# A twelfth 2 MB weight slot, a smaller ring for dynamic DMAs, and a wait moved, in a one-core hybrid decoder step

## The chip, the cores and the metric

The kernel runs on one NeuronCore of a Trainium2 chip. The metric is the device time of one execution in microseconds. A core has TensorE (PE, with its weight loads PEld), VectorE (DVE), ScalarE (ACT), GpSimd (POOL) and SyncE (SP), and 16 DMA engines that all queues share. Here SP starts nearly all the large transfers, and POOL the indirect ones, which gather or scatter rows by a table of numbers (the dynamic DMAs, queue q0).

## The reference, cut to what matters

520 tokens (512 of a prompt, 8 single samples) of width 1024 go through one layer in float32.

```python
z = rmsnorm(x) @ w_in                      # split into xa, ga, ub, vb (512 each)
y_a = gelu(ssm(xa)) * sigmoid(ga)          # state space, 32 groups, complex diagonal state
y_b = gelu(ub) * spatial_gate(rmsnorm(gelu(vb)))
x = x + concat(rmsnorm(y_a), rmsnorm(y_b)) @ w_out
# mixture of experts: one of 4 groups, two of its 8 experts per token
for e in range(32):
    a, u = t @ w_gate[e], t @ w_up[e]      # (1024, 512) each
    out = out + combine[:, e:e+1] * ((silu(a) * u) @ w_down[e])   # (512, 1024)
y = rmsnorm(x + out)                       # plus the new states and the v rows
```

The experts' weights are 32 x 3 x 2 MB = 192 MB, and each of them is read once.

## The kernel before, in words

**Front (to about 241 us).** The projections, the state-space mixer, the gating mixer, the output projection and the router. Its buffers lie in one large tensor `mem`, cut by word offsets: `at_word(at, ...)`, `view(at, ...)` from word 24576 on, and `early` and `small` near the end of it, for the router's tables. Four input weights and two halves of `w_out` pass through slots 6 and 7.

**Weight slots.** `ring` divides the first 45056 words of `mem` into NSLOT = 11 slots of UNIT = 4096 words (16 KB in each of 128 partitions, 2 MB). One unit is half of an expert's gate and up weights, or its whole down weight. `UNITS` lists the 96 units in the order in which PE wants them, and unit q goes into slot q modulo NSLOT. SP loads a slot as soon as the front has left it: units 0 to 5 and 8 with the front's last part, 6, 7, 9 and 10 (in pieces) while the output projection's buffers come free. Unit NSLOT and the one behind it come in pieces as PE has used up slots 0 and 1 (`load_piece`, with the semaphores `gu_part`, `gu_half`, `gu_ps`); from then on `load(q)` waits until PE has used unit q - NSLOT (`gu_half`, `gu_ps` or `dn_ps`).

**Experts.** For each expert in turn, 64 tokens at a time: POOL gathers the tokens' rows from DRAM (`fetch`, two experts ahead), PE turns them, multiplies by gate and up, ACT applies silu, DVE multiplies, PE turns the result and multiplies by down, ACT copies it out, and POOL scatters it to `y2_d` in DRAM (`store`). PE computes expert s's gate and up before expert s - 1's down. Experts with more than 64 tokens take further tiles (`further`). PSUM tensors psA and psB alternate.

**The last two experts** are not scattered: their rows are added by a product with a selection matrix `picks`, which DVE makes once, early (`picks_of`, L1256), from `tokens`, numbers that lie in the same words as ACT's output buffer `yst`. It needs `cw_ps`, a small product that PE does in the middle of expert 1's gate and up. ACT waits for it (`picks_rdy`) before it starts expert 1, and PE before it starts expert 2.

**Zeroes.** `y2_d` is first filled with zeroes, 4 MB, by SP at L368 and L369; ACT waits for that before L627, whose output lies on the zero buffer.

**End.** After the stream, SP reads residuals (`x2f`), scattered rows (`yin`) and the final gain (`gfb`) into slots that are free by then; DVE and PE add and scale, and SP writes the result.

SP runs its waits and its DMA issues strictly in the order of the program. The lines that matter:

```python
def load(q):
    e, j = UNITS[q]
    s = q % NSLOT
    unit(s, (ring[:, s, :], w_dn[e] if j == 2 else w_gu[2 * e + j]))
for q in range(NSLOT + 2, 3 * NE):
    e_old, j_old = UNITS[q - NSLOT]
```

Of the kernel before, what the change touches and what calls it, by code (L numbers as in the profile page):

```python
# [7 lines left out]
D = 1024  # L8
DS = 512
NP_, NS = 512, 8  # L10
NTOK = NP_ + NS
NT = 5
# [14 lines left out]
NSLOT, UNIT = 11, 4096  # L27
FRONT_SLOTS = 6
ARENA = FRONT_SLOTS * UNIT
EPS = 1e-6  # L30
# [11 lines left out]
def build(nc, a, o):  # L42
# [3 lines left out]
    with ctx:  # L46
        def sb(name, shape, dt=f32):
            return ctx.enter_context(nc.sbuf_tensor(name, shape, dt))
# [70 lines left out]
        hnew = at_word(49152, 2, NS, NQ)  # L119
# [68 lines left out]
        thr = small(270, 8)  # L188
        one32 = small(278, NE)
        ex = small(310, NT, NG + 1)  # L190
        row_oh = as_bf16(small(376, NT * C)).rearrange("p (t j c) -> p t j c", t=NT, j=2)
        oh12 = small(696, NT, 2, NE)
        brb = small(336, 36)
# [11 lines left out]
        vi = sb("vi", [128, C])  # L205
        iot = vi[:, :]
        rank_at = early(1160, C)
        ids = cut(1792, 4, 2 * NE)
        ohb = sb("ohb", [128, NT, 32], bf16)
        trib = sb("trib", [128, 128], bf16)  # L210
        oneb = sb("oneb", [128, 128], bf16)
# [4 lines left out]
        picks = small(376, NP_ + 32)  # L216
        tokens = cut(0, NTOK)[64:128]
        x2_root = tiny[:, 0:20].rearrange("p (t w) -> p t w", w=4)
        of_last = small(1016, 2, NT, 2, 2)
        cw3 = as_bf16(small(1056, NT * 2 * 4)).rearrange("p (t j e w) -> p t j e w", t=NT, j=2, e=2)  # L220
        tok_cw = tiny[64:128, 92:96]
        WQ = D // 4
        xq, yq0, yq1, gfq = (at_word(2 * D + WQ * k, WQ) for k in range(4))
        cwq, sumq, rootq, scaleq = tiny[:, 20:22], tiny[:, 22:23], tiny[:, 23:24], tiny[:, 24:25]
        same_row = st[:, 0:32]
# [72 lines left out]
        def as8(s):  # L298
            return ring[:, s, :].rearrange("p (k n) -> p k n", k=KD)

        def as4(s):
            return ring[:, s, :].rearrange("p (k n) -> p k n", k=4)
# [42 lines left out]
        def _(sp):  # L345
            def unit(s, src):
                sp.dma_start(src[0], src[1]).then_inc(w_full[s], 16)
# [6 lines left out]
            unit(7, (ring[:, 7, :], a["w_xa"]))  # L354
            sp.wait_ge(vbp_ps, 1)
            unit(6, (ring[:, 6, :], a["w_ga"]))
            sp.wait_ge(xa_ps, 4)
            unit(7, (ring[:, 7, :], a["w_ub"]))
            sp.wait_ge(ga_ps, 4)
            unit(6, (ring[:, 6, :], a["w_out"][1]))  # L360
# [9 lines left out]
            sp.wait_ge(ub_ps, 4)  # L370
            unit(7, (ring[:, 7, :], a["w_out"][0]))

            def load(q):

                e, j = UNITS[q]
                s = q % NSLOT
                unit(s, (ring[:, s, :], w_dn[e] if j == 2 else w_gu[2 * e + j]))

            def load_blocks(q, k0, k1):

                e, j = UNITS[q]
                s = q % NSLOT
                words = slice(2 * DE * k0, 2 * DE * k1)
                unit(s, (ring[:, s, words], (w_dn[e] if j == 2 else w_gu[2 * e + j])[:, words]))
# [15 lines left out]
            sp.wait_ge(s_ev, NH)  # L400
            sp.dma_start(g2, a["norm2_g"]).then_inc(rest_in, 16)
# [35 lines left out]
            def load_piece(q, n):  # L437

                e, j = UNITS[q]
                s = q % NSLOT  # L440
                k0, k1 = PIECES[s][n]
                sp.dma_start(ring[:, s, 2 * DE * k0:2 * DE * k1],
                             (w_dn[e] if j == 2 else w_gu[2 * e + j])[:, 2 * DE * k0:2 * DE * k1]).then_inc(w_full[s], 16)
# [55 lines left out]
        def _(act):  # L499
# [202 lines left out]
            def tile_step(s, i, u, before=True):  # L702

                ps, other = (psA, psB)[u], (psA, psB)[1 - u]
                x0 = act.value_load(xb[0:1, bass.ds(s, 1)], min_val=0, max_val=NX)
                x1 = act.value_load(xb[0:1, bass.ds(s + 1, 1)], min_val=0, max_val=NX)
                further(x0, x1, other)
                act.wait_ge(gu_ps, s + 1)
                A(sg[64:128, u, :], ps[0:64, 1, :], ACT.Silu, scale=root_of[0:64, u:u + 1]).then_inc(sg_rdy, 1)  # L709
                if before:  # L710
                    tail(s - 1, i, 1 - u)

            def tail(s, n_stored, u):
# [60 lines left out]
        def _(dve):  # L774
# [472 lines left out]
            tile_step(0, 0, early=True)  # L1247
            dve.wait_ge(zero_out, 32)
# [11 lines left out]
            tile_step(1, 1)  # L1260
# [20 lines left out]
            def add_rows(t):  # L1281

                dve.wait_ge(y_in[t], 48 if t < 4 else 64 + 128)
                acc, rows, by = ((x2f[:, t, :], yin[:, 2 * t:2 * t + 2, :], cw[:, :, t]) if t < 4
                                 else (xq, at_word(2 * D + WQ, 2, WQ), cwq))
# [39 lines left out]
        def _(pool):  # L1325
# [8 lines left out]
            def tt(out, x, y, op):  # L1334
# [17 lines left out]
            link(G.memset(trib[:, :], 1.0))  # L1352
            G.memset(oneb[:, :], 1.0)
            G.affine_select(out=trib[:, :], in_=trib[:, :], compare_op=ALU.is_gt, fill=0.0, base=0,
                            pattern=[[1, 128]], channel_multiplier=-1)
            G.iota(iot, [[1, C]], base=0, channel_multiplier=0, allow_small_or_imprecise_dtypes=True).then_inc(iota_rdy, 1)
# [13 lines left out]
            G.memset(zeros, 0.0).then_inc(consts, 1)  # L1370
            pool.wait_ge(st_out, 16 * 5)
# [92 lines left out]
            G.memset(at_word(2 * D, 4 * WQ), 0.0).then_inc(tokens_rdy, 1)  # L1464
# [521 lines left out]
```

## Time and profile before

| | |
|---|---|
| median of 3 runs | 729.3 us (729.06, 729.3, 1117.75) |
| span of the profiled execution | 727.1 us |
| the profiled execution's own time | not recorded apart from its span; the two near runs are 2.0 and 2.2 us above the span |
| PE busy | 652.3 us (90%) |
| DVE, ACT, POOL busy | 255.7, 158.4, 97.2 us |
| moved by DMA | 244.48 MB, of which SP's queue 233.95 MB and the dynamic queue 8.24 MB |

The span runs from the first to the last instruction of the core, and all times in the traces count from its start. The chain of work that ended last passes through PE for 65% of the span, DVE and DMA 11% each. A busy PE is not a bound PE here: the slices of the page show, under PE, how full the DMA engines are, and the two have to be read side by side.

### The profile page before, as it was taken

The page shows a single profiled execution, that of the slowest core. Times are in us where ns is not written, and L with a number is a line of the kernel's source. Part 1 is how long each engine was busy: PE and PEld are TensorE (multiplying, and loading weights), DVE is VectorE, ACT ScalarE, POOL GpSimd, SP SyncE. Part 2 cuts the span into 40 slices and gives each one's busy share as a digit, 9 for nine tenths or more (in the row PEclk, how much of TensorE's full clock was granted, in tenths as well). Part 3 has the DMA queues.
Part 4 walks back from the last instruction along what each step waited for, and adds up shares of the span by engine and source line. Part 5 has one row for each costly group of instructions (what it writes and reads, how often), then busy time and mean ns, then how long its engine had stood idle before and what let it go on. Part 6 is the DMA issues. An engine that isn't in the chain of part 4 may idle for free.

```text
span 727.1 us, 9232 instructions
## 1 busy us (share of the span) xinstructions
PE 652.3 (90%) x3176; PEld 314.2 (43%) x3176; DVE 255.7 (35%) x553; ACT 158.4 (22%) x312; POOL 97.2 (13%) x165
## 2 busy tenths in 40 slices
PE   8999999999999999996899999987777778778994
PEld 5478888874456533332233333322222222223331
DVE  7798997188265612111010101110001100001047
ACT  3677511132322111110011111101001010001123
POOL 5100000000000311222012121212211112121000
PEclk9999999999999899998999999999999999999999
DMA  9532005569848699999999999999999999999993
GB/s 326 222 116 112 5 1 189 184 240 431 300 150 313 208 427 423 425 422 422 428 424 426 424 424 422 425 422 428 422 426 426 426 424 425 425 425 423 411 351 127
DMA packets 32692, 244.48 MB, mean 336 GB/s; under 512 B 7344, under 2 KB 8016, under 8 KB 19584
## 3 DMA queue, kind: packets, MB, share of 16 engines
q1 hardware_dynamic: 25592, 233.95, 78.3%
q0 software_dynamic: 5280, 8.24, 3.1%
q10 hardware_dynamic: 1768, 1.53, 0.7%
q8 instruction: 40, 0.66, 0.4%
q14 instruction: 12, 0.10, 0.0%
HBM read 235.76 MB, written 17.09 MB: 348 GB/s over the span
## 4 chain that ended last, share of the span: by engine, by line
PE 65%; DVE 11%; DMA 11%; another core or an unknown queue 4%; ACT 3%; issue 3%; SPq 1%; ACTq 0%; POOLq 0%; POOL 0%; DVEq 0%
PE psA L1480 33%; PE psB L1480 30%; DMA mem<-in_w_gu 7%; DVE mem L785 4%; DMA mem<-y_d 2%; DVE mem L1009 1%; DMA mem<-x_d,mem 1%; PE psB L1485 1%; ACT front_c L709 1%; DMA y_d<-mem 1%; PE psA L1485 1%; ACT mem L717 1%; DVE mem L924 1%; DVE mem L936 1%
## 5 line engine op out<-in xcount | busy, mean ns | idle before, releaser
L1480 PE MATMUL psA<-mem 128*128 128x260 f32 (+8 forms) x848 | 200.9, 476 | 7.8 <-DMA mem<-in_w_down 5.4
L1480 PE MATMUL psB<-mem 128*64 128x512 f32 (+6 forms) x710 | 153.5, 490 | 13.6 <-DMA mem<-in_w_down 4.7
L1480 PEld LDWEIGHTS psA<-mem 128*128 128x128 f32 (+4 forms) x848 | 108.0, 161 | 82.2 <-issue 61.4
L1480 PE MATMUL psB<-mem,front_c 128*64 128x512 f32 (+3 forms) x554 | 121.5, 577 | 15.9 <-DMA mem<-in_w_gu 15.9
L1480 PE MATMUL psA<-mem,front_c 128*64 128x512 f32 (+2 forms) x548 | 121.1, 581 | 15.5 <-DMA mem<-in_w_gu 13.5
L1480 PEld LDWEIGHTS psB<-mem 128*64 128x64 f32 (+3 forms) x710 | 73.7, 160 | 78.1 <-issue 57.3
L1480 PEld LDWEIGHTS psB<-mem,front_c 128*64 128x64 f32 (+2 forms) x554 | 41.2, 142 | 94.5 <-issue 67.8
L1480 PEld LDWEIGHTS psA<-mem,front_c 128*64 128x64 f32 (+1 forms) x548 | 40.6, 142 | 93.0 <-issue 69.5
L1184 DVE SCALAR_TENSOR_TENSOR front_c<-psA,tiny,front_c 64x512 f32<-64x512 f32 x16 | 12.1, 755 | 180.7 <-ACT front_c L709 168.0
L785 DVE TENSOR_TENSOR mem<-mem 128x512 f32<-128x512 f32 (+15 forms) x109 | 65.5, 615 | 23.8 <-ACT mem L616 19.6
L1184 DVE SCALAR_TENSOR_TENSOR front_c<-psB,tiny,front_c 64x512 f32<-64x512 f32 x16 | 12.1, 755 | 173.3 <-ACT front_c L709 166.6
L1392 POOL DMA_INDIRECT y_d<-front_c,mem x30 | 30.9, 1031 | 263.2 <-ACT front_c L720 263.2
L1387 POOL DMA_INDIRECT mem<-x_d,mem x34 | 36.5, 1072 | 92.4 <-DVE mem L785 64.4
L709 ACT ACTIVATE front_c<-psA,tiny 64x512 f32<-64x512 f32 x15 | 10.2, 682 | 119.2 <-PE psA L1480 119.2
L709 ACT ACTIVATE front_c<-psB,tiny 64x512 f32<-64x512 f32 x15 | 10.2, 682 | 114.8 <-PE psB L1480 114.8
L1485 PE MATMUL psA<-ident,mem 128*128 128x128 f32 (+1 forms) x128 | 19.1, 283 | 5.1 <-DMA mem<-x_d,mem 4.8
L720 ACT ACTIVATE front_c<-psA 128x512 f32<-128x512 f32 x15 | 9.0, 597 | 61.7 <-PE psA L1480 61.7
L720 ACT ACTIVATE front_c<-psB 128x512 f32<-128x512 f32 x15 | 9.0, 597 | 60.3 <-PE psB L1480 60.3
L1485 PEld LDWEIGHTS psA<-ident,mem 128*128 128x128 f32 (+1 forms) x128 | 13.9, 144 | 9.8 <-issue 7.7
L785 DVE TENSOR_TENSOR mem<-psB,mem 128x512 f32<-128x512 f32 (+2 forms) x23 | 15.0, 706 | 2.4 <-PE psB L1480 2.4
L1480 PE MATMUL psB<-ident 128*128 128x128 f32 x60 | 12.4, 391 | 3.0 <-POOL mem L1340 2.0
L1485 PE MATMUL psB<-ident,mem 128*128 128x128 f32 (+1 forms) x88 | 13.5, 279 | 1.7 <-DVE mem L1184 1.7
(260 smaller groups left out, 381.6 us busy)
## 6 DMA issues: line engine op xcount, KB each, us to landing
mem<-in_w_gu SPq DMA_DIRECT2D x61, 2048.0 KB, 35.2
mem<-in_w_down SPq DMA_DIRECT2D x30, 2048.0 KB, 37.5
mem<-in_w_out SPq DMA_DIRECT2D x2, 2048.0 KB, 8.4
y_d<-mem SPq DMA_DIRECT2D x1, 4096.0 KB, 11.8
mem<-y_d SPq DMA_DIRECT2D x8, 512.0 KB, 8.4
mem<-in_w_gu SPq DMA_DIRECT2D x6, 512.0 KB, 3.9
mem<-in_w_down SPq DMA_DIRECT2D x3, 1024.0 KB, 6.2
mem<-in_w_gu SPq DMA_DIRECT2D x3, 1024.0 KB, 7.1
```

Of the source, the lines that this page charges most:

```text
L709: A(sg[64:128, u, :], ps[0:64, 1, :], ACT.Silu, scale=root_of[0:64, u:u + 1]).then_inc(sg_rdy, 1)
L717: A(hT[:, u, :, :], ps[:, 2, 0:256].rearrange("p (k c) -> p k c", k=4), ACT.Copy).then_inc(hT_ev, 1)
L720: A(yst[:, u, :], ps[:, 3, :], ACT.Copy).then_inc(y_cp, 1)
L785: return V.tensor_tensor(out, x, y, op)
L924: V.tensor_copy(*u_copy(ql, e, 1))
L936: ins = V.scalar_tensor_tensor(v[:, hs], v[:, hs], st[0:r, 44 + 4 * t + h:45 + 4 * t + h], gmg[0:r, hs], ALU.mult, ALU.mult)
L1009: V.tensor_copy(mixA[32 * ql:32 * ql + 32, :, 0:NP_].rearrange("p m (b i) -> p i m b", i=T)[:, i], yg[32 * i:32 * i + 32, ql, :, NS:YC])
L1184: return V.scalar_tensor_tensor(out, up, root, silu, ALU.mult, ALU.mult)
L1387: return G.indirect_dma_start(out=dst, out_offset=None, in_=x2_d[:, :], in_offset=bass.IndirectOffsetOnAxis(ap=rows_ap, axis=0), bounds_ch ...
L1392: return G.indirect_dma_start(out=y2_d.rearrange("t (h n) -> (t h) n", h=2), out_offset=bass.IndirectOffsetOnAxis(ap=rows_ap, axis=0), in_ ...
L1480: return nc.tensor.matmul(out, lhsT, rhs, start=start, stop=stop, skip_group_check=True)
L1485: return nc.tensor.transpose(out, in_, ident[b0:b0 + p, b0:b0 + p])
```

## The change

NSLOT becomes 12. The twelfth slot (number 11) is not next to the others: it lies at word 49296, behind the tables, so `ring` becomes a list. Its 4096 words come from three sources: the software ring for dynamic DMAs is set to 2048 bytes of each partition (before, the default of 16384), some separate tensors (`st`, `vi`, `ohb`, `trib`, `oneb`) go into words of `mem` that are free at their time, and the tables are laid closer. The words of slot 11 hold `st` and `hnew` until the new state has been written out; then SP loads unit 11 there, right behind the zeroes and before the second half of `w_out`. What is pieced now are units 12 and 13. POOL makes `trib`, `oneb` and `iot` later, when `dec` is no longer used. DVE makes the selection after its step of expert 1 and not before, and ACT waits for it only before its first write of `yst`. SP waits for `h0_rdy` before it loads the router's biases. The buffers of the end move to slots 1 to 4; before, they lay in slots 8 to 10 and 0, and both sets hold units 85 to 88.

```diff
-NSLOT, UNIT = 11, 4096
+NSLOT, UNIT = 12, 4096
+LAST_SLOT = 49296
+RING_BYTES = 2048
-        mem = sb("mem", [128, ARENA + 24928])
-        ring = mem[:, 0:NSLOT * UNIT].rearrange("p (s n) -> p s n", n=UNIT)
+        mem = sb("mem", [128, LAST_SLOT + UNIT])
+        ring = [mem[:, at:at + UNIT] for at in [UNIT * s for s in range(NSLOT - 1)] + [LAST_SLOT]]
-        hnew = at_word(49152, 2, NS, NQ)
+        hnew = at_word(LAST_SLOT + 64, 2, NS, NQ)
-        gfb = at_word(0, D)
-        y_kept = at_word(D, D)
-        x2f = at_word(8 * UNIT, 4, D)
-        yin = at_word(9 * UNIT, 8, D)
+        gfb = at_word(4 * UNIT, D)
+        y_kept = at_word(4 * UNIT + D, D)
+        x2f = at_word(UNIT, 4, D)
+        yin = at_word(2 * UNIT, 8, D)
-        st = sb("st", [128, 64])
+        st = at_word(LAST_SLOT, 64)
...
@@ sync
             sp.dma_start(y2_d[1024:2 * NTOK, :], zeros[0:2 * NTOK - 1024]).then_inc(zero_out, 16)
-            sp.wait_ge(ub_ps, 4)
-            unit(7, (ring[:, 7, :], a["w_out"][0]))
...
+            sp.wait_ge(st_out, 16 * 5)
+            load(NSLOT - 1)
+            sp.wait_ge(ub_ps, 4)
+            unit(7, (ring[7], a["w_out"][0]))
...
             sp.wait_ge(s_ev, NH)
+            sp.wait_ge(h0_rdy, 2)
             sp.dma_start(g2, a["norm2_g"]).then_inc(rest_in, 16)
@@ scalar
-            def tile_step(s, i, u, before=True):
+            def tile_step(s, i, u, before=True, ahead=None):
...
                 stored(act, n_stored, u)
+                if ahead:
+                    act.wait_ge(*ahead)
                 A(yst[:, u, :], ps[:, 3, :], ACT.Copy).then_inc(y_cp, 1)
...
             tile_step(0, 0, 0, before=False)
-            act.wait_ge(picks_rdy, 1)
-            tile_step(1, 0, 1)
+            tile_step(1, 0, 1, ahead=(picks_rdy, 1))
@@ vector
             tile_step(0, 0, early=True)
+            tile_step(1, 1)
             dve.wait_ge(zero_out, 32)
             dve.wait_ge(tokens_rdy, 1)
             dve.wait_ge(cw_ps, 1)
...
             picks_of(0)
             picks_of(1).then_inc(picks_rdy, 1)
-            tile_step(1, 1)
             tile_step(2, 0)
@@ gpsimd
-            link(G.memset(trib[:, :], 1.0))
-            G.memset(oneb[:, :], 1.0)
...
             pool.wait_ge(s_ev, NH)
             G.memset(zeros, 0.0).then_inc(consts, 1)
+            pool.wait_ge(dec_used, 4)
+            link(G.memset(trib, 1.0))
+            G.memset(oneb, 1.0)
...
-    nc = bacc.Bacc("TRN2", target_bir_lowering=False, num_devices=1)
+    nc = bacc.Bacc("TRN2", target_bir_lowering=False, num_devices=1, dynamic_dma_scratch_size=RING_BYTES)
```

How SP's queue stands around the zeroes, before (`out` are the results, `y_d` is `y2_d`, `in_w_out` and `in_w_gu` weights):

```order
L366 DMA out<-mem 128x128
L368 DMA y_d<-mem 128x8x1024 [waits consts]
L369 DMA y_d<-mem 16x1024
L347 DMA mem<-in_w_out 128x4096 [waits ub_ps]
L401 DMA tiny<-in_norm_g 128x8 [waits s_ev]
L402 DMA mem<-in_b_router_group 128x4
L403 DMA mem<-in_b_router_expert 128x32
```

and in the changed kernel:

```order
L367 DMA out<-mem 128x128
L369 DMA y_d<-mem 128x8x1024 [waits consts]
L370 DMA y_d<-mem 16x1024
L348 DMA mem<-in_w_gu 128x4096 [waits st_out]
L348 DMA mem<-in_w_out 128x4096 [waits ub_ps]
L405 DMA tiny<-in_norm_g 128x8 [waits h0_rdy,s_ev]
L406 DMA mem<-in_b_router_group 128x4
L407 DMA mem<-in_b_router_expert 128x32
```

One weight load of 2 MB has come between the zeroes and `w_out`; it waits for `st_out`, which `w_out` is now behind too.

SP's queue where the slots are used for the second time, before (`gu_part`, `gu_half`, `gu_ps` and `dn_ps` count what PE has used):

```order
L347 DMA mem<-in_w_gu 128x1024 [waits xg_in0,x2_out]
L442 DMA mem<-in_w_gu 128x1024 [waits gu_part] x2
L442 DMA mem<-in_w_gu 128x2048 [waits gu_half]
L442 DMA mem<-in_w_gu 128x2048 [waits gu_part]
L442 DMA mem<-in_w_gu 128x2048 [waits gu_ps]
L347 DMA mem<-in_w_down 128x4096 [waits gu_half]
L347 DMA mem<-in_w_gu 128x4096 [waits gu_ps]
```

and in the changed kernel:

```order
L348 DMA mem<-in_w_gu 128x1024 [waits xg_in0,x2_out]
L446 DMA mem<-in_w_gu 128x1024 [waits gu_part] x2
L446 DMA mem<-in_w_gu 128x2048 [waits gu_half]
L446 DMA mem<-in_w_down 128x2048 [waits gu_part]
L446 DMA mem<-in_w_down 128x2048 [waits gu_ps]
L348 DMA mem<-in_w_gu 128x4096 [waits gu_half]
L348 DMA mem<-in_w_gu 128x4096 [waits gu_ps]
```

The waits stand as before, and behind each stands the unit that came one place later: the down unit of expert 3 where the second gate and up unit of expert 4 was, and so on to the end, which is one load shorter.

DVE's queue in experts 0 and 1, before: the selection (from the row that waits for `cw_ps`) stands right behind expert 0's product (the row that waits for `sg_rdy`):

```order
L1184 SCALAR_TENSOR_TENSOR front_c<-psA,tiny,front_c 64x512 [waits sg_rdy]
L1251 CAST tiny<-mem 64x2 [waits cw_ps,tokens_rdy,zero_out]
L1252 TENSOR_REDUCE tiny<-psB 64x2
L1256 TENSOR_SCALAR mem<-front_c,tiny 64x520 [waits dve_step]
L1256 TENSOR_SCALAR mem<-front_c,tiny 64x520
L1216 TENSOR_LOAD xb
```

and in the changed kernel, from expert 1's product on:

```order
L1189 SCALAR_TENSOR_TENSOR front_c<-psB,tiny,front_c 64x512 [waits sg_rdy]
L1199 COPY tiny<-mem 128x1 [waits xgT_ps]
L790 TENSOR_TENSOR front_c<-psA,tiny 128x512
L1257 CAST tiny<-mem 64x2 [waits cw_ps,tokens_rdy,zero_out]
L1258 TENSOR_REDUCE tiny<-psB 64x2
L1262 TENSOR_SCALAR mem<-front_c,tiny 64x520 [waits dve_step]
L1262 TENSOR_SCALAR mem<-front_c,tiny 64x520
L1221 TENSOR_LOAD xb
```

The selection's four rows have moved behind expert 1's product and behind the turned tokens of expert 2.

## Rows read from the trace of the kernel before

**Rows 1.** page, part 2: DMA share in tenths, GB/s; 40 slices
```profile
DMA  9532005569848699999999999999999999999993
GB/s 326 222 116 112 5 1 189 184 240 431 300 150 313 208 427 423 425 422 422 428 424 426 424 424 422 425 422 428 422 426 426 426 424 425 425 425 423 411 351 127
```

**Rows 2.** windows: stretch, length, busy us by engine (instructions), clock, DMA share, GB/s
```profile
136.00:144.00 8.00, 8.00 (x39) 6.92 (x38) 1.31 (x2) 1.13 (x2) 0.00 (x0) 1.00 0.01 2
...
241.00:246.00 5.00, 4.26 (x41) 3.40 (x42) 3.64 (x16) 0.00 (x0) 0.78 (x2) 0.78 0.41 119
246.00:250.00 4.00, 4.00 (x22) 1.39 (x20) 2.34 (x14) 0.00 (x0) 1.23 (x2) 1.00 0.69 201
250.00:682.00 432.00, 376.73 (x1796) 133.29 (x1794) 53.82 (x105) 52.51 (x95) 77.33 (x126) 0.98 1.01 424
```

**Rows 3.** windows: PE ahead of the weight stream, and behind it
```profile
262.00:330.00 68.00, 66.92 (x328) 23.54 (x324) 9.45 (x21) 8.91 (x16) 14.89 (x26) 1.00 1.01 425
...
500.00:676.00 176.00, 137.68 (x646) 48.00 (x644) 19.05 (x36) 19.16 (x35) 29.13 (x46) 0.99 1.01 425
```

**Rows 4.** waits of PE, 262:460: total us, times, longest
```profile
PE psA L1485 <- DMA mem<-x_d,mem: 4.8, 1, 4.8
```

**Rows 5.** waits of PE, 500:676
```profile
PE psB L1480 <- DMA mem<-in_w_gu: 16.5, 12, 2.5
PE psA L1480 <- DMA mem<-in_w_gu: 11.5, 10, 1.4
```

**Rows 6.** timeline of SP: start us, us, line, transfer
```profile
123.93 0.58 SPq L369 DMA_DIRECT2D y_d<-mem  x1
144.16 0.33 SPq L347 DMA_DIRECT2D mem<-in_w_out  x1
...
241.42 0.33 SPq L347 DMA_DIRECT2D mem<-in_w_gu  x1
246.12 7.07 SPq L442 DMA_DIRECT2D mem<-in_w_gu  x5
...
643.22 4.24 SPq L347 DMA_DIRECT2D mem<-in_w_down  x1
```

**Rows 7.** DMA queues (packets, MB), issues (KB each, us to landing)
```profile
q0 software_dynamic: 5280, 8.24, 3.1%
...
mem<-in_w_gu SPq DMA_DIRECT2D x61, 2048.0 KB, 35.2
...
y_d<-mem SPq DMA_DIRECT2D x1, 4096.0 KB, 11.8
...
mem<-x_d,mem POOLq DMA_INDIRECT x34, 8.9
...
y_d<-front_c,mem POOLq DMA_INDIRECT x30, 8.1
```

**Rows 8.** timeline of ACT: the first that waits for the zeroes
```profile
147.58 1.28 ACT L627 ACT_TABLE_LOAD   x1
```

**Rows 9.** timeline of POOL: its memset, then the rank table
```profile
122.53 0.95 POOL L1370 MEMSET mem<- 128x1024 f32 x1 [49.03 <-DVE mem L785]
173.40 0.16 POOL L1374 IOTA mem<- 128x32 f32 x1 [49.92 <-ACT mem L627]
```

**Rows 10.** timeline of DVE: selection rows, then expert 2's tokens
```profile
257.13 1.12 DVE L1256 TENSOR_SCALAR mem<-front_c,tiny 64x520 f32<-64x520 f32 x2
...
261.93 0.69 DVE L785 TENSOR_TENSOR front_c<-psA,tiny 128x512 f32<-128x512 f32 x1
```

**Rows 11.** timeline of PE: expert 0's down product
```profile
261.40 3.65 PE L1480 MATMUL psA<-mem 128*64 128x512 f32 x16 [0.22 <-ACT mem L717]
```

**Rows 12.** timeline of PE and POOL: last weight wait, last scatter
```profile
672.92 3.65 PE L1480 MATMUL psB<-mem 128*64 128x512 f32 x16 [1.46 <-DMA mem<-in_w_gu]
...
684.56 0.97 POOL L1392 DMA_INDIRECT y_d<-mem  x1 [15.28 <-ACT mem L700]
...
693.57 0.10 POOL L1474 MEMSET mem<- 128x1 int32 x1 [7.92 <-DMA y_d<-mem]
```

More of the change, by code:

```diff
@@ L187, in build @@
         Wp, Wq, Wr, Wm = (small(226 + 10 * k, NT, 2) for k in range(4))
[L188 to L193, printed above, removed]
+        thr = early(1400, 8)
+        one32 = early(1304, NE)
+        ex = early(1372, NT, NG + 1)
+        row_oh = as_bf16(small(268, NT * C)).rearrange("p (t j c) -> p t j c", t=NT, j=2)
+        oh12 = small(588, NT, 2, NE)
+        brb = early(1336, 36)
         xxg = at_word(46088, ROW)
@@ L215, in build @@
         ylast = y_kept[64:128]
-        picks = small(376, NP_ + 32)
+        picks = small(268, NP_ + 32)
         tokens = cut(0, NTOK)[64:128]
         x2_root = tiny[:, 0:20].rearrange("p (t w) -> p t w", w=4)
-        of_last = small(1016, 2, NT, 2, 2)
-        cw3 = as_bf16(small(1056, NT * 2 * 4)).rearrange("p (t j e w) -> p t j e w", t=NT, j=2, e=2)
+        of_last = early(1224, 2, NT, 2, 2)
+        cw3 = as_bf16(early(1264, NT * 2 * 4)).rearrange("p (t j e w) -> p t j e w", t=NT, j=2, e=2)
         tok_cw = tiny[64:128, 92:96]
         WQ = D // 4
-        xq, yq0, yq1, gfq = (at_word(2 * D + WQ * k, WQ) for k in range(4))
+        xq, yq0, yq1, gfq = (at_word(4 * UNIT + 2 * D + WQ * k, WQ) for k in range(4))
         cwq, sumq, rootq, scaleq = tiny[:, 20:22], tiny[:, 22:23], tiny[:, 23:24], tiny[:, 24:25]
-        same_row = st[:, 0:32]
+        same_row = early(1408, 32)
         psA = ctx.enter_context(nc.psum_tensor("psA", [128, 4, 512], f32))
@@ L298, in as8 @@
         def as8(s):
-            return ring[:, s, :].rearrange("p (k n) -> p k n", k=KD)
+            return ring[s].rearrange("p (k n) -> p k n", k=KD)
         def as4(s):
-            return ring[:, s, :].rearrange("p (k n) -> p k n", k=4)
+            return ring[s].rearrange("p (k n) -> p k n", k=4)
         def by_pair(ps):
@@ L353, in _ @@
                 sp.dma_start(x2[0:ROWS[t], t, :], xsrc(t)).then_inc(x_in[t // 3], 16)
-            unit(7, (ring[:, 7, :], a["w_xa"]))
+            unit(7, (ring[7], a["w_xa"]))
             sp.wait_ge(vbp_ps, 1)
-            unit(6, (ring[:, 6, :], a["w_ga"]))
+            unit(6, (ring[6], a["w_ga"]))
             sp.wait_ge(xa_ps, 4)
-            unit(7, (ring[:, 7, :], a["w_ub"]))
+            unit(7, (ring[7], a["w_ub"]))
             sp.wait_ge(ga_ps, 4)
-            unit(6, (ring[:, 6, :], a["w_out"][1]))
+            unit(6, (ring[6], a["w_out"][1]))
             sp.wait_ge(vbn, NT)
@@ L376, in load @@
                 s = q % NSLOT
-                unit(s, (ring[:, s, :], w_dn[e] if j == 2 else w_gu[2 * e + j]))
+                unit(s, (ring[s], w_dn[e] if j == 2 else w_gu[2 * e + j]))
+            sp.wait_ge(st_out, 16 * 5)
+            load(NSLOT - 1)
+            sp.wait_ge(ub_ps, 4)
+            unit(7, (ring[7], a["w_out"][0]))
             def load_blocks(q, k0, k1):
@@ L383, in load_blocks @@
                 words = slice(2 * DE * k0, 2 * DE * k1)
-                unit(s, (ring[:, s, words], (w_dn[e] if j == 2 else w_gu[2 * e + j])[:, words]))
+                unit(s, (ring[s][:, words], (w_dn[e] if j == 2 else w_gu[2 * e + j])[:, words]))
             def reuse_tile(n):
@@ L441, in load_piece @@
                 k0, k1 = PIECES[s][n]
-                sp.dma_start(ring[:, s, 2 * DE * k0:2 * DE * k1],
+                sp.dma_start(ring[s][:, 2 * DE * k0:2 * DE * k1],
                              (w_dn[e] if j == 2 else w_gu[2 * e + j])[:, 2 * DE * k0:2 * DE * k1]).then_inc(w_full[s], 16)
@@ L710, in tile_step, with tail @@
                 if before:
-                    tail(s - 1, i, 1 - u)
-            def tail(s, n_stored, u):
+                    tail(s - 1, i, 1 - u, ahead)
+            def tail(s, n_stored, u, ahead=None):
                 ps = (psA, psB)[u]
@@ L1370, in _ @@
             G.memset(zeros, 0.0).then_inc(consts, 1)
+            pool.wait_ge(dec_used, 4)
+            link(G.memset(trib, 1.0))
+            G.memset(oneb, 1.0)
+            G.affine_select(out=trib, in_=trib, compare_op=ALU.is_gt, fill=0.0, base=0,
+                            pattern=[[1, 128]], channel_multiplier=-1)
+            G.iota(iot, [[1, C]], base=0, channel_multiplier=0, allow_small_or_imprecise_dtypes=True).then_inc(iota_rdy, 1)
             pool.wait_ge(st_out, 16 * 5)
@@ L1463, in _ @@
             pool.wait_ge(dn_ps, NE - 3)
-            G.memset(at_word(2 * D, 4 * WQ), 0.0).then_inc(tokens_rdy, 1)
+            G.memset(at_word(4 * UNIT + 2 * D, 4 * WQ), 0.0).then_inc(tokens_rdy, 1)
             store(NE - 3, NE // 2 - 2, 1)
```

14 lines of the change are left out of this document (5 added, 9 removed).

## The prediction

> **What bounds the kernel now.** I read the slices of the page first. The DMA engines are full from the fourteenth slice on, at 422 to 428 GB/s [rows 1]. Before that they have gaps, two of them nearly empty slices. The windows give the same in us: from 250 to 682 us the engines move 424 GB/s without a gap [rows 2]. This is the stream of the experts' weights.
>
> Then I asked who waits for whom. Between 262 and 330 us PE is busy for 66.92 of 68 us [rows 3], and between 262 and 460 us its longest wait is one gather of 4.8 us; no weight stands in that answer ahead of it [rows 4]. PE lives on the slots that were filled before 241 us. Between 500 and 676 us it is busy for 137.68 of 176 us [rows 3], and of the 38.3 us left, 16.5 + 11.5 = 28.0 us are waits for gate and up weights [rows 5], most of the rest for down weights. So the stock of full slots is used up on the way, and from there each expert ends when its weights land. The last such wait ends at 672.92 us [rows 12]. What follows is a fixed tail of 727.1 - 672.9 = 54.2 us: two experts' products, the last scatter, which lands at 693.57 us [rows 12], the rows read back, the sum.
>
> That makes a short sum: end = start of the stream + bytes left at that time / 424 GB/s + tail. Only bytes moved before the stream starts, in time when the engines idle, take anything off it.
>
> **The twelfth slot.** It takes 2 MB (2.097 MB) out of the stream and moves it ahead. In the stream they cost 2.097 MB / 424 GB/s = 4.95 us [rows 2]; by the slices' 422 and 428 GB/s, 4.97 and 4.90 us [rows 1]. What do they cost in the new place? SP now issues the load after the zeroes, so at 123.93 + 0.58 = 124.5 us or a little later, when the small results have landed. The 4 MB of zeroes take 11.8 us from issue to landing [rows 7], until 135.7 us. From 136 to 144 us the engines move 2 GB/s: 8 us of idle time [rows 2]. The load needs 4.95 of them and is done by about 140.7 us. The next user, the second half of w_out, is issued at 144.16 us [rows 6], when the engines are empty again. Even if the wait for the results held the load until 139.2 us, it would fit. If reads and zeroes share the engines, the zeroes are late by at most 4.95 us, at 140.7 us; ACT, which waits for them, comes to that point at 147.58 us [rows 8], 6.9 us later. So this costs 0 at the lower end. The upper end, if cover were missing altogether, is the 4.95 us themselves; I take 0, because the idle row is measured at just this place.
>
> The Trainium skill has another rate (DMA: Bandwidth & Descriptors, "Where 436 GB/s comes from"): for HBM to SBUF it puts the limit at about 358 GB/s for a core. By that the unit would be worth 2.097 / 358 = 5.9 us, an estimate, and the time 723.4 us. The trace disagrees, with 424 GB/s over 432 us, and the measurement decides; the rule gets no chance of its own.
>
> **The restart of the stream.** The engines also idle from 241 to 246 us (119 GB/s) and are half loaded to 250 us (201 GB/s) [rows 2]. The extra slot does not fill this: it has long been full, and the first reuse waits, as before, for PE's first products of expert 0. SP's first piece went out at 246.12 us, right behind the last prefetch at 241.42 us [rows 6]. Gates, sizes and order of the issues are the same, each with the next unit. Cost and gain 0; the remaining stream is one load shorter.
>
> **Does PE follow?** It has 38.3 us of waiting between 500 and 676 us [rows 3] and needs to give back 4.95 us. The wait for expert 30's weights at 672.92 us moves to about 668.0 us, and the tail with it. SP's last load, now at 643.22 us [rows 6], and the rest of the stream move by the same amount, so the tail meets the same traffic as before.
>
> **The selection for the last experts.** DVE's two large rows take 1.12 us [rows 10], with the two small ones ahead of them I take 1.5 us. Before, they stood in a time when DVE waited for ACT. Now they follow expert 2's turned tokens, which end at 261.93 + 0.69 = 262.62 us [rows 10], so they end near 264.1 us. PE waits for them before expert 2, but until 261.40 + 3.65 = 265.05 us it does expert 0's down product [rows 11]: cover of about 0.9 us. ACT needs them before its copy of that same product, also after 265.05 us. Nothing is queued behind them on DVE that is needed before expert 2's gate and up end. Cost 0. If the cover were gone, a us or two of PE would be lost at a time when PE is ahead of the weights [rows 3, 4], which is made good later. I see no gain either, since the selection was done at 257.13 + 1.12 = 258.25 us [rows 10], before ACT had expert 1's products.
>
> **POOL's tables.** Four small instructions move to behind POOL's memset, which starts at 122.53 us and takes 0.95 us; POOL then waits 49.92 us, until 173.40 us [rows 9], and the first DVE reader also needs what POOL makes after that. They stand behind the zero buffer's memset, so SP's zeroes are not late. Cost 0. SP's wait for h0_rdy asks for something done before the results are written. Cost 0. The moved buffers of the end hold units 85 to 88 as before. Cost 0.
>
> **The smaller ring.** 5280 packets [rows 7] over 34 gathers, 30 scatters and 2 further ones are 80 a DMA, 5 for each of the 16 engines. Per expert one gather (8.9 us to landing) and one scatter (8.1 us) are in flight [rows 7] in the 3 x 4.95 = 14.8 us that its weights take, so 17.0 / 14.8 = 1.15 on average, and hardly over 3. The trace of before shows nothing of how much room a DMA takes in the ring, so I bound it. The lower end is 0. The upper end is the rival on the ring, below. I take 0, because 3 DMAs of 5 packets an engine are little for 2048 bytes on each partition.
>
> The Trainium skill speaks of this ring in SBUF — State Buffer, "SBUF size: 192, 224, or 256?": 16 KiB of each partition are set aside for it. It gives no smaller size that is safe. By DMA: Bandwidth & Descriptors ("Why small descriptors are slow"), a descriptor is 16 B; 2048 bytes would then hold 128 of them, and three DMAs need 15, an estimate that agrees with taking 0. No run here shows it yet.
>
> **Sum.** The profiled execution: 727.1 - 4.95 = 722.15 us of span. The two near runs lie 2.0 and 2.2 us over it, and the median is 729.3 us; against it, 729.3 - 4.95 = **724.4 us**, 0.7% less. With the bounds of the rate and the spread of the runs this case alone covers 723.4 to 725.6 us.
>
> **The rivals.**
> *A gain that is only half there.* The load in its new place gets in somebody's way: it holds up the zeroes or w_out, or the stream starts later by part of what it saved. Half of 4.95 us gone gives 726.8 us. Against it: the idle 8 us [rows 2] and the 6.9 us to ACT's wait.
> *Hidden anyway.* If the end hung on PE's own work, or on the gathers, and the weight waits were only slack, the bytes would be worth nothing: 729.3 us. For it: PE is 90% busy over the span. Against it: the waits of rows 5 end only 54 us before the end, and nothing but DMA ends them.
> *Slower: the ring is too short.* Place: POOL's indirect DMAs in the stream. If a DMA's descriptors can be written only when those of the one before have been used up, gather and scatter run one after the other: 8.9 + 8.1 + 2 x 1.0 us of issue [rows 7, 12] = 19.0 us an expert against 14.8 us. That is 4.2 us for each of some 29 experts, 122 us, and 729.3 - 5 + 122 = 846 us. It decides from the point where fewer than two DMAs fit, since with two in flight the pair takes 9.5 us and hides under the weights. Against it: 5 packets an engine and DMA.
>
> **Chances.** Forecast 0.77, half a gain 0.08, hidden anyway 0.10, ring too short 0.04, and 0.01 for something much faster. The range 722.4 to 727.4 us takes in the forecast and the half gain, 0.85 with their edges counted a little down; the other cases are outside. About 2% is what a measurement of this kernel can tell from no change, and 2% of 729.3 is 14.6 us: the forecast and both neighbours are well within. Faster by more 0.01, within 0.95, slower by more 0.04.
>
> **What would show it.** Right: SP issues a weight load near 124.5 us; the window 136:144 goes from 2 GB/s to over 200; the first piece still goes out near 246 us; the selection's two rows stand near 263 us with no PE wait behind them; PE's waits for weights shrink by about 5 us in total; the last one ends near 668 us; the span is near 722 us. Wrong: ACT's L627 or the front's later stages start later than before (half a gain); the last weight wait is earlier but the end is not (hidden anyway); POOL's gathers and scatters take longer than about 1 us each or PE waits often for x_d (ring). A window in the stream below 420 GB/s would break the rate on which the sum rests.

## The result and the profile after

The kernel with twelve slots takes **723.4 us** (median; 723.3 to 724.3 us in four runs) against 729.2 us. The ratio, from which one run of the kernel before at 1117.75 us is left out, is 0.9928, 95% interval [0.9914, 0.9943], so 5.3 us less [4.2, 6.3]; the two medians are 5.8 us apart, which lies inside that interval. The prediction put 2% as what can be told from no change. The same kernel measured again differed by far less (0.9995 [0.9986, 1.0004], below), so these 0.7% stand clear. The profiled executions have spans of 721.5 and 727.1 us. The forecast was 724.4 us, with a range of 722.4 to 727.4 us.

The windows of the kernel after, at the places of [rows 2] and one stretch more (columns as there):

```profile
136.00:144.00 8.00, 8.00 (x38) 6.95 (x37) 1.31 (x2) 1.13 (x2) 0.00 (x0) 1.00 0.57 240
241.00:246.00 5.00, 4.21 (x46) 2.68 (x46) 4.46 (x20) 0.00 (x0) 1.11 (x3) 1.00 0.44 122
246.00:250.00 4.00, 4.00 (x21) 1.34 (x18) 1.99 (x12) 0.00 (x0) 1.05 (x1) 1.00 0.88 278
...
250.00:676.00 426.00, 375.19 (x1790) 133.35 (x1788) 53.37 (x104) 52.51 (x95) 77.33 (x126) 0.98 1.01 424
```

The idle 8 us now carry 240 GB/s x 8 us = 1.92 MB where 2 GB/s stood; the remaining 0.2 MB of the unit moved before 136 us, among the last zeroes. The stream runs at the same 424 GB/s. From 246 to 250 us there is a difference that the change does not account for, 278 instead of 201 GB/s; I come back to it.

SP's timeline, to be read against [rows 6] (start us, us, line, transfer):

```profile
124.08 0.58 SPq L370 DMA_DIRECT2D y_d<-mem  x1
124.70 1.17 SPq L348 DMA_DIRECT2D mem<-in_w_gu  x1
...
144.29 0.33 SPq L348 DMA_DIRECT2D mem<-in_w_out  x1
...
241.58 0.33 SPq L348 DMA_DIRECT2D mem<-in_w_gu  x1
245.18 2.90 SPq L446 DMA_DIRECT2D mem<-in_w_gu  x3
250.21 2.04 SPq L446 DMA_DIRECT2D mem<-in_w_down  x2
...
637.89 4.24 SPq L348 DMA_DIRECT2D mem<-in_w_down  x1
```

The new load stands at 124.70 us, w_out 0.13 us later than before, the last load 5.33 us earlier (637.89 against 643.22 us).

The landing of the 4 MB of zeroes (us from issue), the windows around it and around the end of the new load, and ACT's first step that waits for the zeroes, against [rows 7] and [rows 8]:

```profile
y_d<-mem SPq DMA_DIRECT2D x1, 4096.0 KB, 12.6
```

```profile
134.00:136.00 2.00, 2.00 (x11) 1.72 (x10) 0.00 (x0) 0.00 (x0) 0.00 (x0) 1.00 1.18 299
136.00:138.00 2.00, 2.00 (x11) 1.74 (x10) 0.08 (x1) 0.71 (x2) 0.00 (x0) 1.00 0.97 410
138.00:140.00 2.00, 2.00 (x11) 1.74 (x10) 1.23 (x2) 0.41 (x1) 0.00 (x0) 1.00 0.94 401
140.00:142.00 2.00, 2.00 (x11) 1.74 (x10) 0.00 (x0) 0.00 (x0) 0.00 (x0) 1.00 0.33 139
```

```profile
147.72 1.28 ACT L631 ACT_TABLE_LOAD   x1
```

The load is done shortly after 140 us, ahead of `w_out` at 144.29 us.

PE's waits from 500 to 671 us (total us, times, longest), the window of the same stretch, and PE's last wait for a weight, against [rows 5], [rows 3] and [rows 12]:

```profile
PE psB L1486 <- DMA mem<-in_w_gu: 14.9, 12, 1.5
PE psA L1486 <- DMA mem<-in_w_gu: 12.2, 9, 2.7
PE psA L1486 <- DMA mem<-in_w_down: 5.6, 5, 1.3
PE psB L1486 <- DMA mem<-in_w_down: 4.7, 5, 1.2
```

```profile
500.00:671.00 171.00, 133.66 (x624) 46.20 (x620) 17.45 (x33) 18.10 (x33) 29.15 (x46) 0.99 1.01 425
```

```profile
667.55 1.94 PE L1486 MATMUL psB<-mem 128*64 128x512 f32 x8 [1.47 <-DMA mem<-in_w_gu]
```

These four rows are also the whole of PE's weight waits from 262 us on, 37.4 us. Before there were 42.0 us, since the first ones stood ahead of 500 us. The first wait for a weight behind expert 0's start, in the trace before and then in the trace after:

```profile
480.85 5.35 PE L1480 MATMUL psA<-mem,front_c 128*64 128x512 f32 x16 [2.00 <-DMA mem<-in_w_gu]
```

```profile
501.39 3.65 PE L1486 MATMUL psA<-mem,front_c 128*64 128x512 f32 x16 [0.75 <-DMA mem<-in_w_gu]
```

So in this pair the twelfth slot does not shorten each wait. PE runs on its stock for 20.5 us longer, 4.6 us of waits never arise, and the last wait ends at 667.55 instead of 672.92 us. How long the stock lasts and what the waits sum to also depend on how fast PE itself runs, and the same kernel differs in both. Profiled again, the kernel before had its first wait at 474.05 us and 44.7 us of weight waits, the kernel after 491.23 and 39.8 us. Among the experiments below, the changed kernel with its selection in the old place has 42.9 us of waits, more than the kernel before, and still its last wait ends at 668.42 us: from 250 to 676 us its PE is busy for 370.17 us, where the kernel after shows 375.19. The sum of the waits is therefore no measure of the gain; the time of the last one is a better one.

The moved rows, on POOL, DVE and PE (start, duration, line; the last bracket is the idle time ahead and what ended it):

```profile
122.68 0.95 POOL L1370 MEMSET mem<- 128x1024 f32 x1 [49.02 <-DVE mem L790]
...
124.79 0.18 POOL L1376 IOTA mem<- 128x64 f32 x1
173.54 0.17 POOL L1380 IOTA mem<- 128x32 f32 x1 [48.57 <-ACT mem L631]
```

```profile
260.99 0.69 DVE L790 TENSOR_TENSOR front_c<-psA,tiny 128x512 f32<-128x512 f32 x1
...
261.98 1.12 DVE L1262 TENSOR_SCALAR mem<-front_c,tiny 64x520 f32<-64x520 f32 x2
```

```profile
260.47 3.65 PE L1486 MATMUL psA<-mem 128*64 128x512 f32 x16 [0.21 <-ACT mem L721]
263.95 1.46 PE L1486 MATMUL psA<-mem,front_c 128*64 128x512 f32 x6
```

POOL still idles 48.57 us after its tables. The selection ends at 263.10 us, PE is busy with expert 0's down product until 264.1 us, and the next product carries no wait.

### The profile page after: what moved, and what is told of

The parts are those of the page before. It is cut to its first block, busy times and chain, and to the rows that moved or that the text cites. A ratio compares the mean times of both kernels' runs of the same rounds, so it can differ in the third digit from the quotient of the medians.

```text
span 721.5 us, 9234 instructions
## 1 busy us (share of the span) xinstructions
PE 650.2 (90%) x3176; PEld 312.9 (43%) x3176; DVE 255.6 (35%) x553; ACT 158.5 (22%) x312; POOL 97.8 (14%) x165
## 4 chain that ended last, share of the span: by engine, by line
PE 64%; DMA 12%; DVE 12%; another core or an unknown queue 4%; ACT 3%; issue 3%; SPq 1%; POOLq 0%; POOL 0%; DVEq 0%
PE psA L1486 33%; PE psB L1486 29%; DMA mem<-in_w_down 7%; DVE mem L790 5%; DMA mem<-y_d 2%; DVE mem L1014 1%; DMA mem<-in_w_vb 1%; DMA mem<-x_d,mem 1%; ACT front_c L713 1%; DMA y_d<-mem 1%; PE psB L1491 1%; PE psA L1491 1%; ACT mem L721 1%; DVE mem L929 1%
## 5 line engine op out<-in xcount | busy, mean ns | idle before, releaser
L1486 PE MATMUL psA<-mem 128*128 128x260 f32 (+9 forms) x863 | 201.5, 470 | 10.4 <-DMA mem<-in_w_down 5.6
L1486 PE MATMUL psB<-mem 128*64 128x512 f32 (+8 forms) x715 | 156.4, 495 | 13.7 <-DMA mem<-in_w_down 4.7
L1486 PEld LDWEIGHTS psA<-mem 128*128 128x128 f32 (+5 forms) x863 | 108.8, 159 | 85.5 <-issue 63.2
L1486 PE MATMUL psB<-mem,front_c 128*64 128x512 f32 (+3 forms) x554 | 119.5, 570 | 12.3 <-DMA mem<-in_w_gu 12.3
L1486 PEld LDWEIGHTS psB<-mem 128*64 128x64 f32 (+5 forms) x715 | 74.5, 162 | 80.1 <-issue 59.2
L790 DVE TENSOR_TENSOR mem<-mem 128x512 f32<-128x512 f32 (+17 forms) x114 | 65.9, 596 | 23.7 <-ACT mem L620 19.6
L1486 PE MATMUL psB<-ident 128*128 128x128 f32 x60 | 10.9, 356 | 3.0 <-POOL mem L1345 2.0
## 6 DMA issues: line engine op xcount, KB each, us to landing
y_d<-mem SPq DMA_DIRECT2D x1, 4096.0 KB, 12.6
```

What stands on the lines that cost most here:

```text
L790: return V.tensor_tensor(out, x, y, op)
L1486: return nc.tensor.matmul(out, lhsT, rhs, start=start, stop=stop, skip_group_check=True)
```

## The experiments

Three groups of kernels ran on three chips, with 24, 17 and 9 runs of the kernel before beside them (728.7, 728.3 and 727.7 us). "Last wait" is the time at which PE's last wait for a weight ends in the profiled execution.

**The pair again.** No edits.

> The kernel before once more, unchanged, to see how its profiled execution varies. Theory A (the 5.6 us between the two spans are 4.95 us of head start and about 0.9 us of PE clock, which differs from execution to execution): the time is the same as before within 0.2%, and the first piece of the stream goes out anywhere from 245.2 to 246.2 us, late where PE is granted half its clock for longer after 236 us. Theory B (the clock is a property of the kernel, so of the change): again 246.1 us, with half the clock from 236.3 to about 243 us.

> The changed kernel once more. Theory A: ratio 0.992 to 0.994 to before; span 721 to 722.5; low clock of another length than the 2.7 us seen. Theory B: span 721.5 and low clock again from 237.3 to 240.4 us, as in the first profile.

Before: ratio 0.9995 [0.9986, 1.0004]. After: 0.9933 [0.9920, 0.9946], that is 4.9 us less [3.9, 5.8]; spans 725.9 and 722.1 us, last waits 671.97 and 668.08 us. The repeated spans are 3.8 us apart where the first ones were 5.6 us apart, and SP's first reload in the kernel before went out at 244.56 us, earlier still than the 245.2 us that I had given as its earliest. The forecast of 4.95 us lies between, and the question is what moves a single execution by a microsecond. The windows from 237 to 243 us show it. First the kernel before as first profiled, then the same kernel again (clock is the number ahead of the last two):

```profile
237.00:240.00 3.00, 2.66 (x12) 2.67 (x13) 2.68 (x17) 1.71 (x3) 1.41 (x2) 0.50 0.42 172
240.00:243.00 3.00, 3.00 (x16) 3.00 (x15) 2.58 (x8) 0.00 (x0) 1.78 (x2) 0.50 0.43 95
```

```profile
237.00:240.00 3.00, 3.00 (x17) 3.00 (x18) 2.72 (x14) 1.71 (x3) 1.90 (x2) 0.58 0.35 116
240.00:243.00 3.00, 2.68 (x35) 2.31 (x33) 2.76 (x10) 0.00 (x0) 1.29 (x2) 0.85 0.44 93
```

The granted clock is at its lower level (0.50, 1.2 GHz) through all of 240 to 243 us in the one, and only at the beginning in the other: PE makes 35 products there instead of 16 (20 of the 35 are small ones, 128x34, which the other execution comes to only at 243.67 us). PE then comes to expert 0 at 243.44 instead of 245.00 us, and SP's first reload goes out at 244.56 instead of 246.12 us. The kernel is the same in both. The first profile of the kernel after had the short stretch, its repetition the long one:

```profile
240.00:243.00 3.00, 2.69 (x22) 2.46 (x21) 2.79 (x10) 0.00 (x0) 1.93 (x2) 0.86 0.45 88
```

```profile
240.00:243.00 3.00, 3.00 (x16) 3.00 (x16) 2.46 (x8) 0.00 (x0) 1.66 (x2) 0.50 0.44 92
```

Paired by the length of this stretch, the last waits are 4.84 us apart (long: 672.92 and 668.08 us) and 4.42 us apart (short: 671.97 and 667.55 us).

**Twelve slots without the head start.** Everything of the change but the early load; unit 11 comes in pieces at the restart, as before. Each later load also waits for the unit eleven places ahead (the last lines of the edit), so one of the twelve slots is always empty: this kernel has the room and the layout, but no deeper stock at any time.

```diff
-            load(NSLOT - 1)                 # behind st_out
...
-            load_piece(NSLOT, 0)
+            load_piece(NSLOT - 1, 0)
...
-            for q in range(NSLOT + 2, 3 * NE):
-                e_old, j_old = UNITS[q - NSLOT]
+            for q in range(NSLOT + 1, 3 * NE):
+                e_old, j_old = UNITS[q - NSLOT + 1]
```

> The changed kernel with all its parts (12 slots, small ring, moved selection, moved tables), but unit 11 is not loaded ahead: it is issued in pieces from PE's first products on, at the moments at which the kernel before issued it, and each later unit waits for the use of the unit 11 places ahead. The twelfth slot is there and is empty at the start. Head-start theory: the gain is gone, 729.2 us (728.3 if the 0.9 us of clock belong to the change's other parts), the last weight wait near 672.5 us. Rival (the room itself or the other parts give the gain): 723.5 us.

Ratio 0.9995 [0.9986, 1.0004]; 136:144 us back at 2 GB/s, last wait 672.00 us.

```profile
136.00:144.00 8.00, 8.00 (x40) 6.95 (x39) 1.31 (x2) 1.18 (x3) 0.00 (x0) 1.00 0.01 2
```

The ring, the tables, the moved buffers and the moved selection together bring at most 1.0 us and cost at most 0.3 us (the ends of the interval). Whether a twelfth slot that is used, but gets no early bytes, is worth something, this run can't say; the next ones bear on it.

**Half of the load ahead.** The other 1 MB is issued behind unit 13's second piece.

```diff
-            load(NSLOT - 1)
+            load_blocks(NSLOT - 1, 0, 2)
...
             load_piece(NSLOT + 1, 1)
+            load_blocks(NSLOT - 1, 2, 4)
```

> The changed kernel with only half of unit 11 (1 MB) loaded ahead, at the same place; the other half goes out in the full stream, behind unit 13. Head-start theory: half of the 4.95 us, so 726.7 us from 729.2 (726.0 if 0.7 us are something else that the change brings). Rival (the head start is not in proportion to bytes, but one unit's wait less): 724 or 729.

Ratio 0.9971 [0.9960, 0.9982], 2.1 us less [1.3, 2.9]; 104 GB/s from 136 to 144 us, last wait 671.08 us. Half the bytes give half the gain within the noise (2.45 us lie inside the interval), although here all twelve slots are in use in the stream. The rival with one unit's wait less, 724 or 729 us, is out.

**The same unit in the other gap.** The whole of unit 11 is issued behind the last prefetch, so at 241.8 us, in the time when the engines run at 119 to 201 GB/s.

```diff
-            load(NSLOT - 1)                 # behind st_out
...
             load_blocks(9, 3, 4)
+            load(NSLOT - 1)
```

> The changed kernel with unit 11 issued at the end of the prefetches (about 241.9 us) and not behind the zeroes (124.7 us). Between 241 and 250 us the DMA engines idle for about 3.4 + 2.1 = 5.5 us in the kernel before (119 and 201 GB/s against 424). Theory (any idle time before the stream is full counts the same): the unit takes 4.95 us of it, but pushes the pieces behind it, so nearly the whole gain, 723.4 to 725.5 us. Rival (the place between zeroes and w_out is what counts, later it only delays the next pieces): 728 us or more.

Ratio 0.9955 [0.9941, 0.9970], 3.3 us less [2.2, 4.3]; last wait 669.27 us. I had expected more: 723.4 to 725.5 us against 729.2 is 3.7 to 5.8 us less. Beside it on the same chip, the changed kernel with its selection in the old place has a median of 723.34 us, and this one 724.95 us, and no run of the one reaches into the range of the other (722.29 to 723.94 and 724.20 to 726.28 us). So about a third of the gain is missing. The window shows the gap well filled, which is not yet a full gain:

```profile
246.00:250.00 4.00, 4.00 (x22) 1.48 (x20) 2.06 (x12) 0.00 (x0) 1.24 (x2) 1.00 0.97 403
```

The stream's own first pieces would have used a part of that time; now they come behind the unit.

**The ring alone.** The kernel before with 2048 bytes of ring, no other edit.

> The kernel before with the ring for dynamic DMAs at 2048 bytes a partition, nothing else. Prediction's view: no cost, 729.2 us, gathers 8.9 us and scatters 8.1 us to landing as before. Ring rival: slower, from POOL's indirect DMAs waiting for room, with longer issues than 1.07 us.

Ratio 0.9998 [0.9990, 1.0007]; gathers 8.9 us and scatters 8.2 us to landing, against 8.9 and 8.1 us [rows 7].

**A ring of 512 bytes**, in the changed kernel: `RING_BYTES = 512`.

> The changed kernel with a ring of 512 bytes instead of 2048. A gather or scatter has 5 packets for each DMA engine. If a ring of this size still holds the DMAs that are in flight, or if the room is counted otherwise: ratio 0.9933 to before, gathers 8.9 us and scatters 8.1 us to landing, POOL's issue about 1 us. If two no longer fit, POOL must wait for the first to be used up: an issue takes up to 8 us, PE waits for x_d, and with 19.0 us an expert against 14.8 us the time is up to 840 us; if only the few moments with three in flight are hit, 0.5 to 3 us of the gain are lost.

Ratio 0.9939 [0.9925, 0.9953], the gain as with 2048 bytes; last wait 668.46 us; gathers land in 8.8 us, scatters in 8.1 us. POOL issues a scatter and a gather 2.2 us apart, in 1.04 and 1.06 us, as in every other kernel here:

```profile
502.81 1.04 POOL L1398 DMA_INDIRECT y_d<-front_c,mem  x1 [9.87 <-ACT front_c L726]
503.85 0.20 POOL L1412 COPY mem<-mem 128x1 int32 x1
505.02 1.06 POOL L1393 DMA_INDIRECT mem<-x_d,mem  x1 [0.98 <-POOL mem L1412]
```

Even a quarter of the chosen ring doesn't bring the serial gather and scatter that the slower rival asked for. How short a ring must be to hurt stays open, and so does how its room is counted: no run made a DMA wait for room.

**The selection back in its old place**, in the changed kernel.

```diff
-            tile_step(1, 0, 1, ahead=(picks_rdy, 1))
+            act.wait_ge(picks_rdy, 1)
+            tile_step(1, 0, 1)
...
-            tile_step(1, 1)                 # DVE, ahead of the selection
+            tile_step(1, 1)                 # behind it
```

> The changed kernel with the selection for the last experts made before expert 1 again on DVE, and ACT's wait where it was. Prediction's view: no difference, 723.4 us within 0.2%. Rival (the moved wait saves part of the 0.7 us that the gain is over the forecast): 724 us, with PE or ACT later in experts 1 and 2.

Ratio 0.9931 [0.9917, 0.9945]: as the change itself (0.9933). The move is worth nothing that can be measured.

**PE kept busy through the half-clock stretch.** In the changed kernel ten filler products instead of six, and three behind the last table products.

```diff
-            keep_busy(6)
+            keep_busy(10)
...
+            keep_busy(3)
```

> The changed kernel with 7 more products on the identity (their result is used by nobody) in PE's two gaps near 233.5 and 236.5 us. Clock theory (the time that PE is at half clock near 240 us delays its first expert and so the first reuse of a slot): the clock stays at 1.00 from 233 to 245 us, PE's first expert starts at about 243 to 244 us, and the time is 0 to 0.9 us less than the changed kernel's, 722.5 to 723.4. Rival (the gather sets the start anyway, and the clock is harmless): 723.4 with the full clock. If the added products hold up PE: up to 0.5 us more.

Ratio 0.9941 [0.9927, 0.9954]; last wait 668.22 us. The clock is at 1.00 from 237 to 243 us, yet PE comes to expert 0 only at 244.43 us. That is not the fillers' doing. The front of this execution was late long before them: SP issued `w_out` at 144.66 us, against 144.07 us in the repeated kernel after. Counted from there, PE reaches expert 0 after 99.77 us. It does so after 99.73 to 99.77 us in each of the three profiles with the short low stretch and in the one with the selection in its old place, and after 100.49 to 100.94 us in the seven with a long one. So the held clock saves about 1 us against a long stretch and nothing against a short one, and in the times no gain can be seen.

**2 MB less in the middle of the stream.** The kernel before; the unit with the second half of expert 20's gate and up weights (not its up weights, as the expectation has it) brings only 64 of 4096 words on each partition, so expert 20 is computed with what the slot held before.

```diff
+                if q == 60:
+                    unit(q % NSLOT, (ring[:, q % NSLOT, 0:64], ...[:, 0:64]))
+                    continue
                 load(q)
```

> The kernel before, with eleven slots, in which one weight unit in the middle of the stream (the up weights of expert 20) brings 64 of its 4096 words on each partition and is otherwise left as it was in the slot; so expert 20's result isn't the reference's. This prices 2 MB of the stream where no slot, head start or layout is changed. If the end is set by the bytes left at the restart over 424 GB/s, 2.06 MB less give 4.9 us: ratio 0.9933, the last weight wait of PE near 4.9 us earlier. If the stock of full slots is worth something by itself (PE starved less often because twelve instead of eleven can be ahead), the twelfth slot's 0.993 has a part of that, and this kernel gives clearly less than 4.9 us. If what is taken out of the middle is filled by other waits, the ratio is above 0.997.

Ratio 0.9946 [0.9933, 0.9960], 3.9 us less [2.9, 4.9]; last wait 668.08 us.

```profile
668.08 3.65 PE L1483 MATMUL psB<-mem 128*64 128x512 f32 x16 [1.45 <-DMA mem<-in_w_gu]
```

By its profile that is 4.84 us before the 672.92 us of the kernel before, both with the long half-clock stretch, and equal to the repeated kernel after, 668.08 us. By its times it is 3.9 us; 4.9 us is the interval's edge. Beside it on the same chip, the changed kernel with a ring of 512 bytes takes 723.46 us and this one 723.98 us, with intervals that overlap widely. So 2 MB out of the stream are worth about the same with eleven slots too. That the twelfth slot has a worth of its own beyond the bytes was not seen, though the times alone leave room for some tenths of a us.

**All profiles on one line.** If the end hangs on the bytes alone, then "last wait + bytes moved so far / 424 GB/s" is the same number in every kernel. I summed rate x length over fourteen windows from 120 to 270 us (the rates are rounded to 1 GB/s, which leaves the sum uncertain by 0.08 MB, or 0.2 us):

| kernel | MB, 120 to 270 us | last wait, us | last wait + MB / 0.424 |
|---|---|---|---|
| ring alone | 41.04 | 673.27 | 770.1 |
| before | 41.11 | 672.92 | 769.9 |
| before again | 41.71 | 671.97 | 770.3 |
| without head start | 41.77 | 672.00 | 770.5 |
| half ahead | 42.25 | 671.08 | 770.7 |
| other gap | 42.74 | 669.27 | 770.1 |
| ring of 512 bytes | 43.25 | 668.46 | 770.5 |
| after again | 43.39 | 668.08 | 770.4 |
| PE kept busy | 43.48 | 668.22 | 770.8 |
| after | 43.52 | 667.55 | 770.2 |
| selection back | 43.56 | 668.42 | 771.2 |

Eleven profiles lie within 1.3 us of each other in the last column, while their last waits differ by 5.7 us. The kernel with the shortened load gives 765.3 us, 5.1 us less than the mean of the others (770.4 us); 2.06 MB / 424 GB/s is 4.9 us. The constant says that from 270 us on the engines are never idle in any of these kernels; that the end follows too has to be seen in the spans. What comes after the last wait takes 53.1 to 54.2 us, less where the last wait is late for its bytes (53.3 us with the selection back, 53.1 us with PE kept busy). With the span in place of the last wait, the sum is 823.8 to 824.4 us in all eleven, and 819.4 us with the shortened load, 4.8 us less. The table also tells why the other gap is worth less: by 270 us it is 1.6 MB ahead of the first profile, where the kernels with the unit behind the zeroes are 2.1 to 2.5 MB ahead. And it tells what the 0.6 MB between the two profiles of the kernel before are: the same kernel with another clock near 240 us.

## Why the prediction was right

**The place of the bound**: shown. The end follows the bytes left over 424 GB/s, in the table and with the shortened load. One reading of the page is off by one: the engines are full from the fifteenth slice on, the fourteenth has 208 GB/s [rows 1]. Nothing rests on it, since the sum used the windows. The tail, which I called fixed at 54.2 us, took between 53.1 and 54.2 us. That the bytes are hidden anyway (0.10) is refuted by the same kernel.

**The 4.95 us**: right. After again measured 4.9 us [3.9, 5.8]. The first pair of runs gave 5.3 us and the first pair of profiles 5.4 to 5.6 us. Until 241 us the kernel after is 2.09 MB ahead (33.68 against 31.59 MB, summed as above), which is 4.93 us. The rest of that pair's difference, 0.32 MB by 270 us, is from the clock: by its profile the kernel before came late to expert 0, and the same kernel did not when it was profiled again. The sum against the median stood on two runs, 729.06 and 729.3 us. The 24 later runs of the kernel before lie between 727.36 and 729.53 us, with a median of 728.7 us; from there the same 4.95 us give 723.8 us, which is what the repeated kernel after measured. The 1 us between the forecast of 724.4 us and the first median is thus mostly the starting point, and not the worth of the bytes.

The rate of 424 GB/s held, and with it the answer to the 358 GB/s that I had set beside it. That this other rate gives 723.4 us, the very median measured, is chance: the stream after runs at 424 GB/s too, and the repeated pair is 4.9 us apart, not 5.9. The Trainium skill, Perfetto Trace Analysis, "Roofline" (under "Engine Utilization"), says that 358 GB/s is a core's share when both cores of a pair use the memory, and that one core alone is bounded by its DMA engines at about 435 GB/s. The trace's 424 GB/s, of a kernel on one core, agree with that.

**The new place costs nothing**: right. The zeroes took 12.6 instead of 11.8 us to land, and ACT's first step behind them started at 147.72 instead of 147.58 us, on a front that ran 0.15 us later from 123 us on. The load was done shortly after 140 us, as forecast. The gain that is only half there (0.08) did not come about; it needed the other gap to see one.

**The restart**: I called its cost and gain zero, with the same gates. It is zero for the change (without the head start: 0.9995), but the first piece does not stand firmly at 246 us as I wrote. Over twelve profiles it stood between 244.56 and 246.24 us, in either kernel, and always 1.1 us behind PE's first product of expert 0. Like the tail, this is a term whose size I took from a single execution as if it were fixed.

**PE gives the time back**: the last wait moved as forecast. The sign that I had named for it, weight waits about 5 us shorter in total, came true in each pair of profiles taken together (4.6 us less, then 4.9), but by luck: across the pairs the same two kernels differ by 2.2 or by 7.3 us, and 42.9 us of waits with the selection back go with the full gain. Nor was it where I looked. Between 500 us and the last waits PE idles nearly as long as before (37.3 of 171 us against 38.3 of 176 us); in the first pair the waits ahead of 500 us are those that have gone.

**The selection**: forecast to end at 264.1 us, ended at 263.10 us, because this execution was 0.9 us earlier; the cover was 264.1 - 263.1 = 1.0 us, forecast 0.9 us. Its move is worth nothing either way. **POOL's tables, the moved buffers**: nothing, by the kernel without the head start. **The ring**: nothing, by the ring alone; the slower rival (0.04) is absent, and at 512 bytes still is. The room that one DMA takes, on which the estimate of 15 descriptors stood, was measured by no run.

## What to carry to other kernels

Where a long stream of weights sets the end, count the bytes that are in before it starts to run full: here each MB moved into an idle stretch was worth 1 MB / 424 GB/s = 2.36 us, and the new slot what was loaded into it in such a stretch. A gap directly ahead of the stream gives less, because the stream's own first pieces would have used a part of it. Before a difference of one or two us between two profiles is explained by an edit, profile the old kernel twice: here it differed from itself by 1.2 us of span. And where a part seems late, look first how late everything ahead of it already was.

## What the runs showed of the hardware

- The granted clock of TensorE fell from 1.00 to 0.50 between 235.4 and 237.5 us in ten of twelve profiles, after PE had been busy for only 1.59 to 1.66 of the 3 us from 233 to 236 us. It came back between 240.5 and 240.9 us in three of them and between 242.3 and 243.3 us in the other seven; the same kernel showed both. The long stretch cost about 1 us of PE's way to expert 0 (100.49 to 100.94 us against 99.73 to 99.77 us behind the issue of `w_out`).
- With the selection in its old place the low stretch lay earlier, from about 231 to 235 us. With more fillers PE was busy for 2.55 of the 3 us from 233 to 236 us, and the clock stayed at 1.00. One profile each.
- A smaller ring, 2048 bytes or 512 bytes, changed neither the issue (1.03 us a scatter, 1.07 us a gather) nor the landing time (8.1 to 8.2 us, 8.8 to 8.9 us) of indirect DMAs with 80 packets each.
- A read of 2 MB issued 1.0 us behind 4 MB of zeroes on the same queue hardly held them up: the zeroes landed in 12.6 instead of 11.8 us, and only about 0.2 MB of the read moved before 136 us, at their end. From 136 to 140 us the read then ran at 401 to 410 GB/s.
